# Routers of a two-block model: transposes by column half, the rank table on GpSimd, a gather part ahead of its chunks

## The chip, the cores and the metric

One core of one Trainium2 chip runs the whole program. The metric is the device time of one execution in microseconds, the median of several runs. The program computes a batch of one sequence of 256 tokens with 1024 channels, in float32.

## What is computed

A diffusion-like first block of two layers with experts, and a second block behind it. What matters here is the expert layer, which stands in both layers of the first block:

```python
h = h + m[:, :, 5] * ec_moe(modulate(rms_norm(h, norm2_g[i]), m[:, :, 3], m[:, :, 4]), *moe)
# rms_norm(x, g) = x * rsqrt(mean(x * x) + EPS) * g
# modulate(xn, shift, scale) = xn * (1 + scale) + shift
```

`ec_moe` is expert choice: a softmax over 16 experts gives each token's affinities, each expert takes the 32 tokens that like it most (of 256), runs its gate, up and down matrices (1024 x 1024 each, silu on the gate) over them, and adds the result, weighted by the affinity, to the token's row. The router is the part that ends in the choice: norm, router product, softmax, the 32 largest per expert, and the rank of each chosen token. The rest (attention and convolution in layer 0, a short convolution in layer 1, then forgetting attention, gated linear attention, cross attention and an MLP) is not touched.

## The kernel before

**The stream.** All large weights pass through `ring`, 8 slots of 2 MB in SBUF, in the order of the list `STREAM`. SyncE issues one DMA per chunk (L496 for experts, L471 for the rest) as soon as the chunk 8 places ahead has been used (`chunks_used`). The experts are 192 of its chunks: per layer four groups of four experts, per group 8 chunks of gate, 8 of up, 8 of down. In layer 0 the groups run as four loops of one, with parts of the cross attention's keys and values between them; in layer 1 they are one loop of four.

**The router** (`route(l)`, once on each of TensorE, VectorE and ScalarE) starts when the mixer's output has been added to `h`: `add_gated` (L1243, L1246) adds four quarters, column half 0 of row tiles 0 and 1, then column half 1 of both, and counts `h_ready`. TensorE transposes h (`transposes`, L1895): row tile 0 whole when three quarters are there, then row tile 1 whole after the fourth. `norm_T` counts the column pairs of which both row tiles are there. ScalarE squares both row tiles for the norm (`squares`, L580) and then evicts column pairs 1 and 3 to `xT` with the scale (`transposed`, L593); VectorE writes row tile 0 normed to `rows` (`normed_tile`, L1437), evicts pairs 0 and 2 (L1171), and writes row tile 1 normed. GpSimd turns the sums of squares into inverse roots (`rms`, L1032, L1033). When all of `xT` is there (`normed_columns`), TensorE forms the router products (L2149), four of the 8 column slices at a time in the four row groups of the array; VectorE copies the parts (L1446), TensorE adds them (L2154), VectorE applies the inverse root and the bias (L1449) and takes the maximum (L1452), ScalarE the exponential (L735), VectorE the normalization (L1454, L1455). After another transpose VectorE finds the 32 largest in four rounds (L1462, L1463), and ranks them (L1466, L1467). The rank goes back through TensorE (L2164), and VectorE writes the one-hot lists (`lists`, L1476), first those of group 0 (`mo_lists` 1), then the others, and then the rank table `RA` (L1489, two instructions, `mo_lists` 2), from which TensorE later broadcasts ranks and affinities (L2239), after the gate products of each group.

**A group** (`experts`): TensorE gathers the chosen rows in four parts of two column slices (`gather(b)`, L2219); VectorE evicts parts 0 and 2 (L1502), ScalarE parts 1 and 3 (L746), to `xsT`. The gate products read it: four chunks by `pair_chunk` (L2190), each released singly, two behind part 0 and two behind part 1; then four by `single_step` (L2211), released two at once. On TensorE's queue the order is: parts 0 and 1; chunks 0, 1; part 2; chunks 2, 3; part 3; chunks 4 to 7:

```python
gather(0)
for b in range(4):
    if b < 3:
        gather(b + 1)
    if b % 2:
        pe.wait_ge(sem("mo_xsT_act"), 2 * n + (b // 2 + 1))
    else:
        pe.wait_ge(sem("mo_xsT_dve"), 2 * n + (b // 2 + 1))
    if b < 2:
        for pair in range(2):
            pair_chunk(0, (0, 1), xsT, 0, b, pair)
single_step(0, (0, 1), xsT, 1)
```

**GpSimd's queue** around it: norm steps, loading the gate row, in layer 0 the memory rows (`mem_rows`) and then the memory norm; in layer 1 a wait for the rank table and then the DMA of `final_g` (L1080) into the place of a table that is done with.

## Time and profile before

| | |
|---|---|
| median of 3 runs | 1688.28 us (1686.38 to 1688.96) |
| span of the profiled execution | 1688.5 us |
| TensorE busy | 1483.4 us, 88% |
| TensorE weight load busy | 831.6 us, 49% |
| VectorE / ScalarE / GpSimd busy | 480.6 / 350.1 / 112.1 us |
| DMA | 562.89 MB, mean 333 GB/s over the span |
| mean granted TensorE clock | 0.961 of full speed |

Three runs and the profiled one agree within 0.2%. The page cuts the span into 40 slices of 42.2 us. The DMA's busy share is 9 tenths in nearly all slices of the first 1280 us; it dips in slice 5 (router 0 lies at 219 to 234 us) and in slices 18 and 19 (mixer and router of layer 1, the router at 825 to 841 us), and falls for good at some 1240 us, where the second block begins. TensorE's busy share is 9 nearly throughout, but it includes matmuls that run at half clock and those whose ends are modelled, so it does not say by itself that TensorE is the bound.

### The profile page before, as it was taken

What the parts mean: (1) busy time and instruction counts of PE and PEld (TensorE: products, weight loads), DVE (VectorE), ACT (ScalarE), POOL (GpSimd) and SP (SyncE); (2) the same over time, 40 slices, a digit from 0 to 9 for tenths busy, and PEclk for the clock granted to TensorE, in tenths of its full rate; (3) what the DMA queues carried; (4) which work ended last, traced back from release to release, by engine and by line L of the source; (5) the groups of instructions that cost most, each with busy time, mean ns of one, the idle gap of its engine ahead of it and who ended that gap; (6) DMA issues with size and microseconds to landing.
All of it is one profiled execution on the core that took longest, in us unless ns stands there. A gap on an engine that the chain in (4) does not pass through costs nothing. (4 is left out here: it accounts for less than half of the span.)

```text
span 1688.5 us, 18007 instructions
## 1 busy us (share of the span) xinstructions
PE 1483.4 (88%) x7708; PEld 831.6 (49%) x7708; DVE 480.6 (28%) x732; ACT 350.1 (21%) x523; POOL 112.1 (7%) x109
## 2 busy tenths in 40 slices
PE   4999979789888899789798888978878999999999
PEld 2755642232242243289532322323324867788997
DVE  1487540110100000056600100001003765336453
ACT  1122410000000000043210000000003645544442
POOL 0000000000000000010000000000002044330000
PEclk8999979989989999999899999999999999999999
DMA  9979959999999999995489999999999743334520
GB/s 373 375 316 418 396 199 429 416 402 429 416 428 428 413 409 429 415 392 202 168 364 423 427 429 423 428 428 421 429 427 364 271 168 135 121 128 174 198 100 26
DMA packets 93288, 562.89 MB, mean 333 GB/s; under 512 B 8048, under 2 KB 9448, under 8 KB 53670
## 3 DMA queue, kind: packets, MB, share of 16 engines
q1 hardware_dynamic: 89504, 551.77, 80.5%
q0 software_dynamic: 2384, 9.42, 1.6%
q8 instruction: 51, 0.84, 0.2%
q10 hardware_dynamic: 1334, 0.75, 0.2%
q14 instruction: 15, 0.12, 0.0%
HBM read 558.74 MB, written 3.17 MB: 333 GB/s over the span
## 5 line engine op out<-in xcount | busy, mean ns | idle before, releaser
L2211 PE MATMUL ps<-ring,scratch 128*32 128x512 f32 x2048 | 439.0, 609 | 63.0 <-DMA ring<-in_moe_w_up 29.6
L2211 PEld LDWEIGHTS ps<-ring,scratch 128*32 128x32 f32 x2048 | 130.7, 112 | 358.2 <-issue 351.1
L2190 PE MATMUL ps<-ring,scratch 128*32 128x512 f32 x1024 | 206.5, 607 | 28.2 <-DMA ring<-in_moe_w_down 28.2
L1930 PE MATMUL ps<-ring_parts,scratch_parts 128*128 128x512 f32 x656 | 187.0, 402 | 4.9 <-DVE xT_parts L1192 1.4
L1930 PE MATMUL ps<-scratch_parts,ring_parts 128*128 128x256 f32 x704 | 146.5, 281 | 0.0
L1930 PEld LDWEIGHTS ps<-ring_parts,scratch_parts 128*128 128x128 f32 x656 | 122.2, 189 | 33.4 <-DVE xT_parts L1192 1.6
L2190 PEld LDWEIGHTS ps<-ring,scratch 128*32 128x32 f32 x1024 | 50.6, 111 | 159.8 <-issue 109.9
L610 ACT ACTIVATE ring_parts<-ring 128x2048 fp32r<-128x2048 f32 x56 | 106.3, 1917 | 93.1 <-PE ps L1930 86.7
L461 DVE TENSOR_TENSOR ring_parts<-ring,ring_parts 128x2048 fp32r<-128x2048 f32 x46 | 105.7, 2298 | 54.9 <-ACT ring_parts L610 53.7
L1930 PEld LDWEIGHTS ps<-scratch_parts,ring_parts 128*128 128x128 f32 x704 | 116.4, 189 | 0.3
L1523 DVE TENSOR_TENSOR scratch<-ps,gate_bc 128x512 f32<-128x512 f32 x16 | 11.1, 692 | 256.8 <-PE ps L2190 256.8
L1930 PE MATMUL ps<-xT_parts,ring_parts 128*128 128x256 f32 x288 | 82.2, 286 | 1.3 <-DVE xT_parts L1183 1.3
L2219 PE MATMUL ps<-scratch,rows 128*128 128x128 f32 (+1 forms) x256 | 66.6, 421 | 14.1 <-DVE scratch L1552 5.7
L2219 PEld LDWEIGHTS ps<-scratch,rows 128*128 128x128 f32 x256 | 61.5, 327 | 32.1 <-issue 31.0
L1512 DVE TENSOR_TENSOR scratch<-scratch,ps 128x1024 f32<-128x1024 f32 x8 | 9.8, 1221 | 236.7 <-PE ps L2211 236.7
L1915 PE MATMUL ps<-ring,xT 128*128 128x512 f32 x160 | 72.9, 616 | 2.5 <-DVE xT L1171 2.5
L746 ACT ACTIVATE scratch<-ps,mod_cols,scale_cols 128x128 f32<-128x128 f32 x32 | 12.9, 453 | 276.9 <-PE ps L2219 276.9
L1930 PE MATMUL ps<-ring_parts,xT_parts 128*128 128x512 f32 x160 | 62.9, 393 | 0.0
L1508 DVE SCALAR_TENSOR_TENSOR scratch<-ps,cst,scratch 128x256 f32<-128x256 f32 x8 | 3.9, 483 | 186.9 <-ACT scratch L750 186.9
L1875 PE MATMUL ps<-ring,silu_c 128*32 128x512 f32 x384 | 50.0, 656 | 7.8 <-issue 6.9
L758 ACT ACTIVATE scratch<-ps 128x512 f32<-128x512 f32 x8 | 4.8, 597 | 246.7 <-PE ps L2245 246.7
L1930 PEld LDWEIGHTS ps<-xT_parts,ring_parts 128*128 128x128 f32 x288 | 54.2, 188 | 1.8 <-issue 1.5
(394 smaller groups left out, 1574.0 us busy)
## 6 DMA issues: line engine op xcount, KB each, us to landing
ring<-in_moe_w_gate SPq DMA_DIRECT2D x64, 2048.0 KB, 26.2
ring<-in_moe_w_up SPq DMA_DIRECT2D x64, 2048.0 KB, 15.6
ring<-in_moe_w_down SPq DMA_DIRECT2D x64, 2048.0 KB, 27.1
ring<-in_ada_w SPq DMA_DIRECT2D x24, 2048.0 KB, 14.0
ring<-in_mlp_w SPq DMA_DIRECT2D x16, 2048.0 KB, 8.5
ring<-in_sc_w_in SPq DMA_DIRECT2D x6, 2048.0 KB, 21.2
ring<-in_w_in SPq DMA_DIRECT2D x6, 2048.0 KB, 20.0
ring<-in_xattn_wkv SPq DMA_DIRECT2D x4, 2048.0 KB, 27.4
```

Source lines behind the costliest of these rows:

```text
L461: ops.tensor_tensor(lo, w, hi.bitcast(F32), ALU.subtract).then_inc(sem("w_split"), 1)
L610: nc.scalar.activation(hi, w, ACT.Copy).then_inc(sem("w_high"), 1)
L746: last = nc.scalar.activation(xsT[:, k, :], ps[:, GATHER[b], P * (k % 2):P * (k % 2 + 1)], ACT.Identity, scale=scale[:, k:k + 1], bias=shi ...
L758: nc.scalar.activation(flat(hT[:, 4:8, :]), pb(7), ACT.Copy).then_inc(sem("mo_hT_act"), 1)
L1512: nc.vector.tensor_tensor(hid, hid, ps[:, 2:4, :].rearrange("p b f -> p (b f)"), ALU.mult)\
L1523: nc.vector.tensor_tensor(ym[:, 512 * j:512 * j + 512], pb(4 + j), gate_bc[:, 512 * j:512 * j + 512], ALU.mult).then_inc(sem("mo_ym"), 1)
L1875: last = mm(ps[32 * j:32 * j + 32, bank, :], lhs, rhs, start=(c == k == 0), stop=(c == 3 and k == 1))
L1915: last = mm(ps[:, banks[t], col:col + width], lhs[:, k, P * t:P * (t + 1)], slot8(i)[:, k, 0:width], start=(k == 0), stop=(k == KD - 1))
L1930: last = mm(out, lhs[x], rhs[y], start=start and n == 0, stop=stop and n == 2)
L2190: last = mm(ps[32 * j:32 * j + 32, banks[half], :], src[:, k, CAP * j:CAP * (j + 1)], w[:, e, col:col + 512], start=(k == 0), stop=(k == K ...
L2211: last = mm(ps[32 * j:32 * j + 32, banks[half], :], src[:, k, CAP * j:CAP * (j + 1)], w[e][:, 0, col:col + 512], start=(k == 0), stop=(k = ...
L2219: last = mm(ps[:, GATHER[b], P * (k % 2):P * (k % 2 + 1)], run_slice(rows[:, t, :], k), onehot[:, t, bass.ds(g * P, P)], start=(t == 0), s ...
```

## The change

Four edits. (1) In both routers TensorE transposes by column half: half 0 of both row tiles when `h_ready` has counted two quarters, then half 1; router products of half 0 start when its evictions are done (a new semaphore `router_xT` counts them), those of half 1 wait for the others. (2) ScalarE squares row tile 1 after its evictions, VectorE evicts first, writes row tile 0 normed after that, and row tile 1 normed behind the maximum; the biased logits now wait for the inverse root of row tile 1. (3) The rank table is written by GpSimd (`rank_rows`), behind the first lists; the wait of the broadcast counts it as the third of `mo_lists`. (4) In every group the order on TensorE's queue becomes: part 0; chunks 0, 1; parts 1 and 2; chunks 2, 3; part 3; chunks 4 to 7.

```diff
@@ -571,14 +574,18 @@
+            def row_squares(name, src, junk, t, ready, count):
+
+                u = NORMS.index(name)
+                if ready:
+                    act.wait_ge(sem(ready), count)
+                nc.scalar.activation(junk, src[:, t, :], ACT.Square,
+                                     accum_out=ss[:, u, t:t + 1]).then_inc(sem("norm_ss"), 1)
+
             def squares(name, src, junk, ready=None, first=0, step=1):
...
-                u = NORMS.index(name)
                 for t in range(NT):
-                    if ready:
-                        act.wait_ge(sem(ready), first + step * t)
-                    nc.scalar.activation(junk[:, t, :], src[:, t, :], ACT.Square,
-                                         accum_out=ss[:, u, t:t + 1]).then_inc(sem("norm_ss"), 1)
+                    row_squares(name, src, junk[:, t, :], t, ready, first + step * t)
@@ -594,7 +601,7 @@
                                                         bias=shift[:, k:k + 1])
-                    last.then_inc(sem("xT_ready"), 1)
+                    last.then_inc(sem("router_xT" if name in ("moe0", "moe1") and b < 2 else "xT_ready"), 1)
@@ -728,8 +735,9 @@
                 name = f"moe{l}"
-                squares(name, h, route_junk[l], "h_ready", 4 * l + 3)
+                row_squares(name, h, route_junk[l][0], 0, "h_ready", 4 * l + 3)
                 transposed(name, xT)
+                row_squares(name, h, route_junk[l][1], 1, "h_ready", 4 * l + 4)
                 act.wait_ge(sem("mo_max"), l + 1)
@@ -1023,6 +1031,16 @@
+            def rank_rows(l):
+
+                grp = cst[0:E, C_GRP:C_GRP + GROUPS].unsqueeze(2).broadcast_to([E, GROUPS, N])
+                pool.wait_ge(sem("mo_operand"), 3 * l + 3)
+                pool.wait_ge(sem("mo_lists"), 3 * l + 1)
+                for v, src in ((0, rank), (1, affT)):
+                    last = nc.gpsimd.tensor_tensor(RA[0:E, :, v, :], src[0:E, :].unsqueeze(1).broadcast_to([E, GROUPS, N]),
+                                                   grp, ALU.mult)
+                last.then_inc(sem("mo_lists"), 1)
+
             def rms(name):
@@ -1049,6 +1067,7 @@
             pool.dma_start(mem_rows, a["mem_2"][0].rearrange("(t p) d -> p t d", p=P)).then_inc(sem("mem_in"), 16)
+            rank_rows(0)
             rms("mem")
@@ -1076,7 +1095,7 @@
             load_gate(1, 1)
-            pool.wait_ge(sem("mo_lists"), 3)
+            rank_rows(1)
             pool.dma_start(final_bc, a["final_g"].partition_broadcast(P)).then_inc(sem("final_in"), 16)
@@ -1172,7 +1191,7 @@
                                                            ALU.mult, ALU.add)
-                    last.then_inc(sem("xT_ready"), 1)
+                    last.then_inc(sem("router_xT" if name in ("moe0", "moe1") and b < 2 else "xT_ready"), 1)
@@ -1438,18 +1457,19 @@
                 dve.wait_ge(sem("h_ready"), 4 * (l + 1))
+                transposed(name, xT)
                 normed_tile(0)
-                transposed(name, xT)
-                normed_tile(1)
...
                 dve.wait_ge(sem("mo_logits"), 2 * l + 2)
+                dve.wait_ge(sem("norm_rstd"), 2 * u + 2)
                 for t in range(NT):
...
                 nc.vector.tensor_reduce(sm[:, 130:132], aff, AX.X, ALU.max, negate=True).then_inc(sem("mo_max"), 1)
+                normed_tile(1)
                 dve.wait_ge(sem("mo_exp"), 2 * l + 2)
@@ -1482,13 +1502,8 @@
                 for t in range(NT):
-                    lists(t, EG, E)
-
-                grp = cst[0:E, C_GRP:C_GRP + GROUPS].unsqueeze(2).broadcast_to([E, GROUPS, N])
-                for v, src in ((0, rank), (1, affT)):
-                    ins = nc.vector.tensor_tensor(RA[0:E, :, v, :], src[0:E, :].unsqueeze(1).broadcast_to([E, GROUPS, N]),
-                                                  grp, ALU.mult)
-                ins.then_inc(sem("mo_lists"), 1)
+                    last = lists(t, EG, E)
+                last.then_inc(sem("mo_lists"), 1)
@@ -1883,19 +1898,23 @@
+            def row_columns(name, src, t, ks):
+
+                bank = NORM_BANKS[name]
+                for k in ks:
+                    cols = run_slice(src[:, t, :], k) if name in ("moe0", "moe1") else src[:, t, P * k:P * (k + 1)]
+                    last = nc.tensor.transpose(ps[:, bank[k // 2], 256 * (k % 2) + P * t:256 * (k % 2) + P * (t + 1)],
+                                               cols, ident)
+                    if t == NT - 1 and k % 2:
+                        last.then_inc(sem("norm_T"), 1)
+
             def transposes(name, src, ready="norm_rows", first=None, step=1):
...
-                v, bank = TRANSPOSED.index(name), NORM_BANKS[name]
                 first = 2 * NORMED.index(name) + 1 if first is None else first
...
                         pe.wait_ge(sem(ready), first + step * t)
-                    for k in range(KD):
-                        cols = run_slice(src[:, t, :], k) if name in ("moe0", "moe1") else src[:, t, P * k:P * (k + 1)]
-                        last = nc.tensor.transpose(ps[:, bank[k // 2], 256 * (k % 2) + P * t:256 * (k % 2) + P * (t + 1)],
-                                                   cols, ident)
-                        if t == NT - 1 and k % 2:
-                            last.then_inc(sem("norm_T"), 1)
+                    row_columns(name, src, t, range(KD))
@@ -2142,10 +2161,15 @@
                 name = f"moe{l}"
-                transposes(name, h, "h_ready", 4 * l + 3)
-                normed_columns(name)
+                for half in range(2):
+                    for t in range(NT):
+                        pe.wait_ge(sem("h_ready"), 4 * l + (3 + t if half else 2))
+                        row_columns(name, h, t, range(4 * half, 4 * half + 4))
+                pe.wait_ge(sem("router_xT"), 2 * l + 2)
                 for k in range(KD):
                     j = k % 4
+                    if k == 4:
+                        normed_columns(name)
                     last = mm(ps[32 * j:32 * j + 32, 0, 0:N], lf[:, E * (k + 7 * l):E * (k + 7 * l) + 32], xT[:, k, :],
@@ -2166,7 +2190,7 @@
                 pe.wait_ge(sem("norm_rows"), 2 * NORMED.index(name) + 2)
-                pe.wait_ge(sem("mo_lists"), 2 * l + 1)
+                pe.wait_ge(sem("mo_lists"), 3 * l + 1)
@@ -2224,7 +2248,9 @@
                     for b in range(4):
-                        if b < 3:
+                        if b == 1:
+                            gather(1)
+                        if 1 <= b < 3:
                             gather(b + 1)
@@ -2235,7 +2261,7 @@
-                    pe.wait_ge(sem("mo_lists"), 2 * l + 2)
+                    pe.wait_ge(sem("mo_lists"), 3 * l + 3)
                     mm(pb(4), cst[0:E, C_E4:C_E4 + P], RA[0:E].rearrange("e g v n -> e (g v n)")[:, bass.ds(g * 2 * N, 2 * N)],
```

Left out above: `route_junk` becomes pairs of single-row buffers, and the counts of `xT_ready` are tabled in `COLUMNS_READY`, since two of four evictions of each router now count elsewhere.

## Rows read from the trace of the kernel before

**Rows 1.** Stretches by time: busy us of each engine, clock, DMA share, GB/s.
```profile
860.00:1000.00 140.00, 123.30 (x565) 41.23 (x564) 8.48 (x14) 9.68 (x14) 0.00 (x0) 0.95 1.01 426
...
231.00:243.00 12.00, 9.18 (x44) 5.45 (x46) 6.13 (x13) 0.81 (x2) 0.00 (x0) 0.60 0.04 17
```

**Rows 2.** SyncE's issues in group 0 of layer 0: start, us, line, what.
```profile
243.01 0.33 SPq L496 DMA_DIRECT2D ring<-in_moe_w_up  x1
...
262.19 0.81 SPq L496 DMA_DIRECT2D ring<-in_moe_w_up  x2
```

**Rows 3.** Single issues to landing: 243.0; fifth at 262.2, 388.6, 868.0, 511.6.
```profile
ring<-in_moe_w_up SPq DMA_DIRECT2D x1, 2048.0 KB, 7.8
...
ring<-in_moe_w_up SPq DMA_DIRECT2D x1, 2048.0 KB, 8.8
...
ring<-in_moe_w_up SPq DMA_DIRECT2D x1, 2048.0 KB, 9.0
...
ring<-in_moe_w_up SPq DMA_DIRECT2D x1, 2048.0 KB, 9.7
...
ring<-in_moe_w_up SPq DMA_DIRECT2D x1, 2048.0 KB, 12.0
```

**Rows 4.** Instructions in time order: start, us, what, count, idle before; router 0, router 1.
```profile
219.20 1.06 ACT L580 ACTIVATE rows<-h 128x1024 f32<-128x1024 f32 x1 [1.60 <-DVE h L1246]
219.20 0.75 DVE L1437 TENSOR_SCALAR rows<-h,rstd 128x1024 f32<-128x1024 f32 x1
...
219.22 1.23 PE L1895 MATMUL ps<-cst,h 128*128 128x128 f32 x8 [0.56 <-DVE h L1246]
219.87 1.66 DVE L1171 TENSOR_SCALAR xT<-ps,scale_cols 128x256 f32<-128x256 f32 x4
...
220.26 1.55 ACT L593 ACTIVATE xT<-ps,scale_cols 128x256 f32<-128x256 f32 x4
...
221.86 1.07 PE L2149 MATMUL ps<-xT,router_w 128*32 128x256 f32 x16 [1.41 <-ACT xT L593]
...
224.55 0.38 DVE L1449 SCALAR_TENSOR_TENSOR scratch<-ps,rstd,small 128x16 f32<-128x16 f32 x2 [1.13 <-PE ps L2154]
...
827.83 1.94 PE L2149 MATMUL ps<-xT,router_w 128*32 128x256 f32 x16 [1.41 <-ACT xT L593]
```

**Rows 5.** The same view: GpSimd's last norm step, VectorE behind the exponential, router 0.
```profile
220.71 0.54 POOL L1033 TENSOR_TENSOR rstd<-ms,mhalf 128x1 f32<-128x1 f32 x1
...
225.91 0.17 DVE L1454 RECIPROCAL small<-small 128x2 f32<-128x2 f32 x1 [0.76 <-ACT scratch L735]
```

**Rows 6.** The same view: gather and first chunk in router 0, group 1, router 1.
```profile
234.21 4.07 PE L2219 MATMUL ps<-scratch,rows 128*128 128x128 f32 x16 [1.05 <-DVE scratch L1476]
234.82 2.34 DVE L1489 TENSOR_TENSOR scratch<-scratch,cst 16x1024 f32<-16x1024 f32 x2
237.09 0.71 DVE L1502 TENSOR_SCALAR scratch<-ps,scale_cols,mod_cols 128x128 f32<-128x128 f32 x2
238.21 6.51 PE L2190 MATMUL ps<-ring,scratch 128*32 128x512 f32 x32
...
362.89 0.73 DVE L1502 TENSOR_SCALAR scratch<-ps,scale_cols,mod_cols 128x128 f32<-128x128 f32 x2 [2.37 <-PE ps L2219]
...
841.28 4.00 PE L2219 MATMUL ps<-scratch,rows 128*128 x16 [1.29 <-DVE scratch L1476]
```

**Rows 7.** Stretches at half granted clock (the third number from the end).
```profile
223.40:240.60 17.20, 8.41 (x30) 5.67 (x32) 10.81 (x31) 2.78 (x7) 0.60 (x1) 0.50 0.42 124
...
827.60:844.60 17.00, 7.28 (x38) 5.23 (x39) 11.73 (x32) 3.44 (x7) 1.20 (x2) 0.50 0.35 133
```

**Rows 8.** GpSimd's groups and single instructions, and the broadcast on TensorE.
```profile
L1107 POOL TENSOR_TENSOR scratch<-scratch,gate_bc 128x1024 f32<-128x1024 f32 x1 | 3.6, 3590 | 5.8 <-ACT scratch L897 5.8
...
841.10 0.53 POOL L1080 DMA_DIRECT2D scratch<-in_final_g  x1 [12.83 <-DVE scratch L1476]
...
267.28 1.12 PE L2239 MATMUL ps<-scratch,cst 16*128 16x512 f32 x2
```

More of the change, by code:

```diff
@@ L398, in build @@
         cw1 = gcol[:, 6:6 + SCK, :].rearrange("p j c -> p c j")
+        COLUMNS_READY = {}
+        for name in TRANSPOSED:
+            COLUMNS_READY[name] = sum(2 if n in ("moe0", "moe1") else 4 for n in TRANSPOSED[:len(COLUMNS_READY) + 1])
         PARAMS = 7
```

6 lines of the change are left out of this document (3 added, 3 removed).

## The prediction

> **What bounds the kernel now.** I read the DMA share by stretch first, then the loading queue, then the two routers instruction by instruction. The change touches the two routers and the start of each expert group, so the question is what a microsecond there is worth. Through layer 1's experts the 16 DMA engines are never free: share 1.01 and 426 GB/s over 140 us [rows 1], while TensorE has idle time. A 2048 KB chunk then takes 4.9 us (2.10 MB by 426 GB/s), and TensorE waits for chunks. The stream stands still in one kind of place: a router uses no expert chunk, so once the eight ring slots are full nothing can be loaded. Before 243.0 us the share is 0.04 for 12 us [rows 1]. It starts again when the first gate chunk of group 0 has been used: the queue issues at 243.01 [rows 2]. So a router's length counts only through the moments at which it lets the queue go on, and whatever the stream wins there it keeps, because after it the stream is the bound until late in layer 1.
>
> The first release is not the only such moment. After 243.01 four chunks are released one by one, and the fifth and sixth together at 262.19 [rows 2], because `single_step` counts two at once. Four chunks are 4 x 4.9 = 19.6 us of transfer, and the fifth release comes 19.2 us after the first: the stream is just kept fed. A chunk issued to an empty queue lands 7.8 us later [rows 3]. There are four places where the ring restarts close to empty: router 0, layer 0's groups 1 and 3, router 1. The fifth chunk lands 8.8, 9.0 and 9.7 us after its issue in the first, second and fourth [rows 3], and 8.9 in group 3, which repeats group 1. So in these places the fifth release could come only 1.0, 1.2, 1.1 and 1.9 us later before it delays the stream. I call this the slack; the argument hangs on it.
>
> **The change part by part.** *Router chain, layer 0.* Now ScalarE squares the second row tile (1.06 us) before its two evictions, and VectorE writes a normed tile (0.75) before its own; the evictions end at 221.8 and router products start at 221.86 [rows 4]. In the new order the first column half is transposed and ScalarE evicts its part while the last addition to h is still running; after 219.2 there are left four transposes (half of the 1.23 us), VectorE's four evictions (1.66, started at 219.2 in place of 219.87) and ScalarE's last two (half of 1.55, from 219.9). Evictions end at 220.9, 0.95 earlier, and the first half of the products is done by then, so 0.5 of their 1.07 us goes too. The copy of the partial logits, which now follows the products' end at 222.93, waits for their new end (221.5) and for the normed tile, moved behind the evictions (220.9 + 0.75 = 221.7). Gain 1.3 us. The moved squares start at 220.8 and need their 1.06 us, the read of the sum (0.2) and GpSimd's two steps (until 221.25 after a start at 219.20, 2.05 us in all): the inverse root is there at 222.9. It is first needed by the biased logits at 224.55 - 1.3 = 223.2: hidden by 0.3 us, and each further delay of the squares would cost in full. The second normed tile (0.75) moves into the wait for the exponentials, which is 0.76 long [rows 5]: nothing, at most 0.1. The exp table load follows the squares at 222.1 for 1.28 us and ends before the maximum (223.8): nothing.
>
> *Router chain, layer 1.* The same, but here products run 1.94 us instead of 1.07 [rows 4], since the granted clock falls to half at 827.6 [rows 7]. Starting 0.95 earlier, they end about there and take the short time: 0.95 + 1.94 - 0.55 = 2.3, less 0.1 for the normed tile, 2.2 us. If the clock falls earlier instead it is 1.3 to 1.4.
>
> *Rank table to GpSimd.* It takes two instructions, 2.34 us, off VectorE, directly ahead of the eviction of gather part 0 (237.09) [rows 6]. Now that delay is covered by gather part 1; with the new gather order it would not be, so this part is needed for the next. On GpSimd no row shows this shape; the nearest with a broadcast input is 3.6 us for 128x1024 [rows 8], so 5 to 7.2 us for both, from 234 to about 241. TensorE needs it at 267.3 [rows 8]: free, with 25 us of room. Behind it on GpSimd's queue wait, in layer 0, only the memory norms of group 1. In layer 1 the DMA of final_g moves from 841.1 [rows 8] to about 845, close to the stream's restart: 0.5 MB, 0 to 1.2 us if they meet; I take 0.
>
> *Gather order, every group.* Now: part 0, part 1 (4.0 us together), then the first chunk at 238.21 [rows 6]. New: part 0 (2.05), then nothing to do for TensorE until VectorE has evicted it, 0.73 us as in group 1, where VectorE is free and starts at once [rows 6], then the chunk: 3.0 us after the gather's start instead of 4.0. The first chunk starts 1.0 earlier. Part 1 follows after two chunks, so the third chunk comes 1.1 later and everything behind it 0.85 later (the exposed eviction). The work until the fifth release is the same plus this gap: **the fifth release loses 0.85 us against the gather's start**, where there is 1.0 to 1.9 of slack.
>
> *The clock.* In both routers the gather begins at half clock, and full clock comes back at 240.6, 6.4 us after its start at 234.21 [rows 6, 7], and at 844.6, 3.3 us after 841.28. A gather part takes 2.0 to 2.1 us at either level, but chunks take twice the time at half: now they run cold for 240.6 - 238.2 = 2.4 and 0 us, a loss of 1.2 and 0. In the new order chunks start a microsecond earlier into the cold (0.5 more), and the gap of 0.85 us lies in the midst of the burst that brings the clock back. If the return counts from the work behind the gap (3.3 to 6.4 us after the first chunk) the loss is 1.7 to 3.2, on average 1.9 more than now. Nothing in this trace shows such a gap; the bounds are 0.5 and 3 us, and I take 1.5, between them, for each of the four places. In the other groups the fifth chunk waits in a full queue, 12.0 us from issue to landing in layer 0's group 2 [rows 3] and longer in layer 1's, where the ring is full: 4 us or more of room (12.0 - 7.8), and what TensorE loses there costs nothing.
>
> **The sum.** Change at the fifth release = 0.85 + 1.5 = 2.35 us later against the gather's start; less slack, less what the router chain saved. Router 0: 2.35 - 1.0 - 1.3 = 0.05. Group 1: 2.35 - 1.2 = +1.15. Group 3: 2.35 - 1.1 = +1.25. Router 1: 2.35 - 1.9 - 2.2 = -1.75. Total +0.7 us. The profiled execution's span is 1688.5 us and the median of the runs 1688.28, so no correction is due: 1688.3 + 0.7 = 1689.0. A change that shortens both routers is worth nothing, because the stream is let go by the fifth release and not by the first.
>
> A rule of the Trainium skill, TensorE: Matmul & The Clock Gate (Part 1: The HAM clock gate), speaks against the change: the throttle is the default and only sustained activity releases it, so a hole in the burst is paid at half clock. It also says that the number of cold matmuls differs between runs of one kernel and that the ramp is under 1% of a typical kernel; by it rival B holds, with a scatter that I can't place. DMA: Bandwidth & Descriptors (Anatomy of one DMA) gives a fixed cost of about 2.0 us plus bytes by 436 GB/s, 6.8 us for a lone chunk, for another issuing path; by that the slack would be 1 us larger in each place and the time, as an estimate, 1686. The row shows 7.8 (the same in router 1 and group 3) and decides.
>
> **The rivals.** *A, the router's gain comes through whole.* If the clock comes back at the same moment as now, the fifth release is 1.35 later against the gather (2.15 in router 1, which now has no cold chunk): router 0 -1.0, groups 1 and 3 +0.15 each, router 1 -1.8: 1685.8. If besides the first release governs everywhere (four chunks are enough lead), routers give 1.8 and 1.9 and groups 1 and 3, where the first release finds the queue all but empty too, 0.5 to 0.8 each (1.0 less half of what chunks run longer cold): 5 us, 1683.3. For it: the share is 1.00 between 243 and 262 and there is slack. Against: the slack is smaller than gap and cold chunks together.
>
> *B, the gap holds the clock down (slower).* Full clock then comes 6.4 us after the first chunk: extra 3, at the fifth release 3.85 later: router 0 +1.55, group 1 +2.65, group 3 +2.75, router 1 -0.25: +6.7, 1695.0; with half of the places so, 1691.9. It decides against the change when full clock returns more than some 8.5 us after the gather's start. For it: half clock lasts through 17 us of scattered work in both routers [rows 7]. Against: one gap of 0.85 us is short.
>
> *C, the change does not do what it says:* TensorE may reach the first half late, since its queue still holds the mixer's last products, or the squares reach the biased logits late. Each takes up to 0.5 us of the router gain: 1689.5 to 1690. It stays in the forecast's range.
>
> **How the numbers follow.** Forecast with C 0.70: 1689.0, own range 1686.5 to 1691.5. A 0.15 (its whole form 0.08). B 0.15. The range that leaves out 2 in 10 reaches from A's milder form to B's with half of the places: 1685.2 to 1692.3. A measurement of this kernel can tell some 0.2% (3.4 us) from no change: faster by more needs A's whole form or a router gain beyond my count, 0.12; slower by more needs B, 0.14; within it 0.74.
>
> **What would show it.** Right: router products in two bursts, the partial-logits copy earlier against the last addition to h by 1.3 us in layer 0 and 2.2 in layer 1; an idle time of TensorE of about 0.8 us between gather part 0 and the first chunk; the first `in_moe_w_up` issue 1 to 2 us earlier against the last addition to h, the fifth later against the first by 2.1 to 3.5 us; the landings of the fifth chunk 7.8 to 8 us after its issue. Wrong: a fifth chunk landing 9 us or more after its issue (then the first release governs, A), full clock unchanged against the gather's start (A) or later than 8.5 us (B), a wait of the rank products on GpSimd, or DMA share under 1.00 between restarts.

## The result, and the profile after

The changed kernel is slower by about a quarter of a per cent.

| | before | after |
|---|---|---|
| median of 16 runs each | 1687.76 us (1683.25 to 1689.81) | 1691.72 us (1688.53 to 1693.67) |
| ratio | | 1.0028 (95% interval 1.0020 to 1.0036) |
| span of the profiled execution | 1688.5 us | 1690.1 us |
| last addition to h to gather, router 0 / router 1 | 15.04 / 16.14 us | 13.38 / 13.41 us |
| GpSimd busy | 112.1 us | 120.0 us |
| mean granted TensorE clock | 0.961 | 0.964 |

The forecast was +0.7 us (1689.0). The medians differ by 4.0 us, the ratio is worth 4.7 us. The two profiled spans differ by 1.7 us only, but the profiled execution of after happened to be 1.6 us ahead when router 0 began (last addition to h ending at 217.59 instead of 219.17), so I compare stretches and not positions.

The page of after: its busy times, and the groups of the first gate chunks and of the gather.

```profile
PE 1487.6 (88%) x7708; PEld 829.6 (49%) x7708; DVE 479.7 (28%) x728; ACT 350.5 (21%) x523; POOL 120.0 (7%) x113
...
L2214 PE MATMUL ps<-ring,scratch 128*32 128x512 f32 x1024 | 215.4, 628 | 37.2 <-DMA ring<-in_moe_w_down 30.2
...
L2243 PE MATMUL ps<-scratch,rows 128*128 128x128 f32 (+1 forms) x256 | 66.5, 413 | 14.1 <-DVE scratch L1567 5.7
```

The products of `pair_chunk`, the first behind each gather, take 628 ns each on average; in the kernel before they took 607 (206.5 us in all). More of them run at half clock: 64 of the 1024 take over 1 us, where 20 did before.

Router 0 and the gather behind it, after, in order of time (start, us, engine, line, what, count, idle before). These rows answer [rows 4 to 6].

```profile
216.90 0.69 DVE L1265 TENSOR_TENSOR h<-h,xT 128x512 f32<-128x512 f32 x1
217.19 0.84 ACT L600 ACTIVATE xT<-ps,scale_cols 128x256 f32<-128x256 f32 x2 [1.17 <-PE ps L1906]
217.63 1.66 DVE L1190 TENSOR_SCALAR xT<-ps,scale_cols 128x256 f32<-128x256 f32 x4
...
218.56 1.42 PE L2173 MATMUL ps<-xT,router_w 128*32 128x256 f32 x16 [0.17 <-DVE xT L1190]
...
219.16 1.06 ACT L582 ACTIVATE rows<-h 128x1024 f32<-128x1024 f32 x1
...
220.05 0.42 DVE L1464 COPY scratch<-ps 128x256 f32<-128x256 f32 x1
...
220.53 0.62 PE L2178 MATMUL ps<-small,scratch 128*128 128x16 f32 x4 [0.55 <-DVE scratch L1464]
220.67 0.54 POOL L1051 TENSOR_TENSOR rstd<-ms,mhalf 128x1 f32<-128x1 f32 x1
...
221.32 0.38 DVE L1468 SCALAR_TENSOR_TENSOR scratch<-ps,rstd,small 128x16 f32<-128x16 f32 x2 [0.84 <-POOL rstd L1051]
...
230.25 3.13 DVE L1496 TENSOR_TENSOR scratch<-cst,scratch 128x128 f32<-128x128 f32 x4
230.89 4.24 POOL L1040 TENSOR_TENSOR scratch<-scratch,cst 16x1024 f32<-16x1024 f32 x2 [7.46 <-DVE scratch L1496]
...
230.98 2.20 PE L2243 MATMUL ps<-scratch,rows 128*128 128x128 f32 x8 [1.05 <-DVE scratch L1496]
233.30 0.72 DVE L1517 TENSOR_SCALAR scratch<-ps,scale_cols,mod_cols 128x128 f32<-128x128 f32 x2
...
234.07 7.80 PE L2214 MATMUL ps<-ring,scratch 128*32 128x512 f32 x32 [0.89 <-DVE scratch L1517]
```

What to see: ScalarE begins to evict xT while the last addition to h runs; the copy of the partial logits starts 2.46 us after that addition's end (220.05 - 217.59). Before it was 3.83 after. The two rows of before behind that number, and behind the sum of the parts below:

```profile
223.00 0.42 DVE L1446 COPY scratch<-ps 128x256 f32<-128x256 f32 x1 [0.81 <-PE ps L2149]
...
223.48 1.04 PE L2154 MATMUL ps<-small,scratch 128*128 128x16 f32 x4 [0.55 <-DVE scratch L1446]
```

In the kernel after, TensorE idles 0.89 us between gather part 0 and the first chunk, which starts 3.09 us after the gather. The first two chunks take 7.80 us against 6.51 in [rows 6].

The same two marks in router 1.

```profile
825.99 0.69 DVE L1265 TENSOR_TENSOR h<-h,xT 128x512 f32<-128x512 f32 x1
...
829.14 0.42 DVE L1464 COPY scratch<-ps 128x256 f32<-128x256 f32 x1
...
840.10 2.23 PE L2243 MATMUL ps<-scratch,rows 128*128 x8 [1.28 <-DVE scratch L1496]
```

Again 2.46 us, here against 4.70 before (the copy then started at 829.84, the last addition to h ended at 825.14). From the last addition to h to the gather this pair of executions gives 1.66 and 2.73 us, 4.4 in all. How much router 1 gives depends on the execution of before that it is held against, because the clock does not fall at the same moment in each: in dose1 (below), whose router 1 is the old one, the router products still ran at full clock,

```profile
827.57 1.07 PE L2149 MATMUL ps<-xT,router_w 128*32 128x256 f32 x16 [1.41 <-ACT xT L593]
```

against 1.94 us in [rows 4]. The five kernels with the old routers (before, gather_and_rank, dose1, dose2, dose4) took 14.41 to 15.04 us over router 0 and 14.65 to 16.14 over router 1, means 14.90 and 15.48; the nine with the new ones took 13.37 to 13.43 and 13.41 to 13.62. On average the routers thus gave 1.5 and 2.0 us, 3.5 in all. The loss is in what follows.

Stretches of 6 us around the issue of the fifth chunk (2 us ahead of it to 4 us behind it) in after: router 0, group 1, group 3, router 1. Columns as in [rows 1]; the last two are the DMA share and GB/s.

```profile
259.21:265.21 6.00, 6.00 (x38) 1.83 (x36) 0.00 (x0) 0.00 (x0) 0.00 (x0) 1.00 0.86 325
386.44:392.44 6.00, 6.00 (x38) 1.83 (x36) 0.00 (x0) 0.00 (x0) 0.00 (x0) 1.00 0.90 330
648.08:654.08 6.00, 6.00 (x38) 1.82 (x36) 0.00 (x0) 0.00 (x0) 0.00 (x0) 1.00 0.91 347
867.61:873.61 6.00, 6.00 (x38) 1.83 (x36) 0.00 (x0) 0.00 (x0) 0.00 (x0) 1.00 0.82 319
```

And the same stretch of group 1 in the kernel before:

```profile
386.56:392.56 6.00, 6.00 (x38) 1.82 (x36) 0.00 (x0) 0.00 (x0) 0.00 (x0) 1.00 1.01 431
```

The stream moved 426 GB/s when full [rows 1]. At 325 GB/s, 6 us lack 6 x (1 - 325/426) = 1.42 us of stream; the four rows of after lack 1.42, 1.35, 1.11 and 1.51, mean 1.35. The four stretches of before (426, 431, 431, 421 GB/s) lack nothing, mean 0.0. I call this **the hole**. TensorE is at work in it (6.00 of 6.00 us busy), so TensorE's busy time does not show it. It costs time later, because the stream is the bound.

The issues of after around it, in group 1: the fourth and the fifth chunk, and the landing times after issue.

```profile
378.38 0.33 SPq L499 DMA_DIRECT2D ring<-in_moe_w_up  x1
...
388.44 0.33 SPq L499 DMA_DIRECT2D ring<-in_moe_w_up  x1
...
ring<-in_moe_w_up SPq DMA_DIRECT2D x1, 2048.0 KB, 12.8
...
ring<-in_moe_w_up SPq DMA_DIRECT2D x1, 2048.0 KB, 10.1
```

The fourth chunk lands at 391.2, the fifth at 398.5, 7.3 us later where a full stream takes 4.9. The stretch that lies mostly ahead of the fourth landing, and the one behind it:

```profile
388.50:391.50 3.00, 3.00 (x16) 0.82 (x14) 0.00 (x0) 0.00 (x0) 0.00 (x0) 1.00 0.74 224
391.50:396.00 4.50, 4.50 (x20) 1.13 (x18) 0.48 (x1) 1.30 (x2) 0.00 (x0) 1.00 1.01 415
```

The stream is at half its rate while the fourth chunk is still landing, and full again behind it. The first issue of this group is at 367.39, the fifth 21.05 us behind it; before it was 19.18 behind in all four places.

The third issue comes later as well, 9.2 us behind the first instead of 7.4. Two chunks are 9.8 us of transfer, so by the same reckoning it is still in time, and the 6 us around it lack nothing (426, 429, 421 and 421 GB/s in the four places). Group 1:

```profile
374.63:380.63 6.00, 5.78 (x34) 2.87 (x30) 0.00 (x0) 0.19 (x1) 0.00 (x0) 1.00 1.03 429
```

### The profile page after: what moved, and what is told of

Read it like the earlier page. It is cut to its first block and busy times, and to the rows that moved or that the text cites. A ratio compares the mean times of both kernels' runs of the same rounds, so it can differ in the third digit from the quotient of the medians.

```text
span 1690.1 us, 18009 instructions
## 1 busy us (share of the span) xinstructions
PE 1487.6 (88%) x7708; PEld 829.6 (49%) x7708; DVE 479.7 (28%) x728; ACT 350.5 (21%) x523; POOL 120.0 (7%) x113
## 5 line engine op out<-in xcount | busy, mean ns | idle before, releaser
L2235 PE MATMUL ps<-ring,scratch 128*32 128x512 f32 x2048 | 438.4, 609 | 54.6 <-DMA ring<-in_moe_w_up 24.9
L2214 PE MATMUL ps<-ring,scratch 128*32 128x512 f32 x1024 | 215.4, 628 | 37.2 <-DMA ring<-in_moe_w_down 30.2
L766 ACT ACTIVATE scratch<-ps 128x512 f32<-128x512 f32 x8 | 4.8, 597 | 243.0 <-PE ps L2271 243.0
```

The source lines that it names most:

```text
L766: nc.scalar.activation(flat(hT[:, 4:8, :]), pb(7), ACT.Copy).then_inc(sem("mo_hT_act"), 1)
L2214: last = mm(ps[32 * j:32 * j + 32, banks[half], :], src[:, k, CAP * j:CAP * (j + 1)], w[:, e, col:col + 512], start=(k == 0), stop=(k == K ...
L2235: last = mm(ps[32 * j:32 * j + 32, banks[half], :], src[:, k, CAP * j:CAP * (j + 1)], w[e][:, 0, col:col + 512], start=(k == 0), stop=(k = ...
```

## The experiments

Each ratio is to the kernel before, run beside it. Three marks are read in each of the four places (router 0, groups 1 and 3 of layer 0, router 1) and given as means: the first issue after the gather's start (before 8.39 us), the fifth issue after the first (before 19.18), and the fifth landing after the gather's start (before 36.68; after 38.93). The hole is read as above. The table in the next section has them all. All expectations but the last were written before the hole was understood; "lead" in them is the time from the fifth chunk's issue to the fourth's landing.

**The gather order undone.** After, with edit 4 alone taken back:

```diff
-                        if b == 1:
-                            gather(1)
-                        if 1 <= b < 3:
+                        if b < 3:
                             gather(b + 1)
```

> The changed kernel with the old order of gather parts; router edits and the rank table on GpSimd stay. Theory 1 (the gather order costs, because it moves the fifth release of a group 1.85 us and more against the first, and the stream runs dry in the four places where the ring restarts close to empty): the router chain's 1.6 us (layer 0) and 2.7 us (layer 1), read from the changed kernel's trace, come through whole: 4.3 us faster than before, ratio 0.9974; fifth release 19.2 us behind the first as before. Rival 2 (the router edits or GpSimd's interference cost the time): no faster than before, ratio 1.000 or more.

Measured 0.9977 (0.9967 to 0.9987): 3.9 us faster than before, 8.6 faster than after. The first three edits are a gain and the fourth turns it into a loss. It also speaks against the prediction's sentence that a shorter router is worth nothing: 4.3 us of router (3.5 against the mean of the old routers) became 3.9 us of time.

**Edits 3 and 4 without the others.** Before, with the rank table on GpSimd and the new gather order.

> The kernel before with the new gather order and the rank table on GpSimd, no router edits. Theory 1: all of the loss and none of the gain: 4.0 + 4.3 = 8 us slower than before, ratio 1.005. My prediction's slack (1.0, 1.2, 1.1, 1.9 us, with 2.35 later at the fifth release) would give +4.2 us, 1.0025. Rival 2: within 0.1% of before.

Measured 1.0039 (1.0027 to 1.0052), +6.6 us. Fifth issue 21.04 after the first, fifth landing at 39.10, holes of 1.2 us. The slack model's 1.0025 lies just below the interval.

**The new order in layer 1 only.** After, with `if l == 1` around the new order.

> The changed kernel with the new gather order in layer 1 alone; layer 0 has the old one. Theory 1: of the four places only router 1's is left, where the fifth chunk lands some 2.5 us later against the gather's start; layer 1's other groups have a full ring and pay nothing: 2 to 3 us slower than the changed kernel with the old order everywhere (0.9977), so 0.9990 to 0.9995. If the loss came from every group (TensorE's own time): four of eight groups, half of 7.5 us, 0.9999. If it came from layer 0 alone: 0.9977.

Measured 0.9994 (0.9984 to 1.0003). Group 3 of layer 0 (old order) and router 1 (new order):

```profile
638.32:644.32 6.00, 6.00 (x38) 1.83 (x36) 0.00 (x0) 0.00 (x0) 0.00 (x0) 1.00 1.00 423
...
858.00:864.00 6.00, 6.00 (x38) 1.83 (x36) 0.00 (x0) 0.00 (x0) 0.00 (x0) 1.00 0.91 347
```

One place of four has the new order close to an empty ring, and it alone has the hole (347 GB/s, 1.11 us). The other three groups of layer 1 have the new order too, with a full ring, and their chunks land 4.9 us apart, with 423 to 429 GB/s around the fifth issue: there the order costs nothing, as predicted.

**The routers alone.** After, with the old order and the rank table back on VectorE.

> The changed kernel with the old gather order and the rank table back on VectorE: the router edits alone. Theory 1: the rank table is worth nothing where gather part 1 covers it, on either engine: the same as with the table on GpSimd, 0.9974 to 0.9980. Rival: GpSimd's table doubles the time of the other lists on VectorE (1.0 to 2.7 us in the changed kernel's trace) and that costs in the old order too: this one faster by 1 us or more, under 0.997.

Measured 0.9977 (0.9966 to 0.9987), the same as with the table on GpSimd. With the old gather order it is worth nothing where the table is built; with the new order no run has it on VectorE. It changes how long the lists take, though; VectorE in this kernel:

```profile
228.37 1.43 DVE L1485 TENSOR_TENSOR scratch<-cst,scratch 128x128 f32<-128x128 f32 x4
```

The same four instructions took 3.13 us in after, beside GpSimd's table. All of the difference is in the fourth, which starts 0.24 us behind GpSimd's first product:

```profile
231.13 2.25 DVE L1496 TENSOR_TENSOR scratch<-cst,scratch 128x384 f32<-128x384 f32 x1
```

In router_only it takes 0.55 us. GpSimd's two products take 2.07 us (beside this list) and 2.19 (the second runs on for 1.7 us after the list's end), so VectorE is what is slowed. The gather waits for the first list only; in after the fourth ends at 233.38, where the eviction of gather part 0 begins, so a longer one would have delayed the first chunk.

**More work between the first and the fifth release.** Before, with half of gather part 3 multiplied once more next to part 3 (dose 1), or all of it (dose 2, `(0, 1)` for `(0,)`); the values written are those that stand there.

```diff
                     for b in range(4):
+                        if b == 2:
+                            gather(3, (0,), False)
                         if b < 3:
                             gather(b + 1)
```

> The kernel before; half of gather part 3 (one column slice) is multiplied twice in every group: the fifth release comes 1.05 us later against the first. Slack as I predicted it (1.0, 1.2, 1.1, 1.9): it swallows the delay, 0 to 0.1 us slower, ratio 1.000. No slack (the fifth chunk must be issued 3.9 us or more before the fourth lands, and before it just was): landings of the fifth chunk 1 us later in the four places, 4 us slower, ratio 1.0025.

> The kernel before; gather part 3 of every group is multiplied twice (the same products into the same place), so that the fifth release comes 2.1 us later against the first, and nothing before it moves. Slack as I predicted it (1.0, 1.2, 1.1, 1.9): +1.1 +0.9 +1.0 +0.2 = 3.2 us slower, ratio 1.0019. Theory 1 in its sharper form (no slack; a chunk issued while the previous one is in its last 3 us leaves a hole of up to 2.5 us, as in the changed kernel's trace at 388 and 870 us): 2.1 to 2.5 us in each of four places, 8.4 to 10 us slower, ratio 1.005 to 1.006.

Measured 1.0016 (1.0004 to 1.0028) and 1.0043 (1.0031 to 1.0055). Both lie above the slack model (1.000 and 1.0019), though this edit makes no gap, leaves the routers alone and does not move the third issue (7.37 us behind the first, as before). So the slack was wrong, whatever the gap does to the clock. Group 1 of dose 1 and of dose 2:

```profile
385.16:391.16 6.00, 6.00 (x38) 1.83 (x36) 0.00 (x0) 0.00 (x0) 0.00 (x0) 1.00 0.98 377
```
```profile
386.40:392.40 6.00, 6.00 (x38) 1.83 (x36) 0.00 (x0) 0.00 (x0) 0.00 (x0) 1.00 0.95 358
```

**The wait that holds the fifth release, moved.** The fifth and sixth chunks are multiplied with all four column slices of parts 2 and 3; only the last two need part 3's eviction. In the kernel with the gather order undone, the wait goes there:

```diff
                                 for kk in range(RUN):
+                                    if c0 == 0 and pair == half == 0 and kk == 2:
+                                        pe.wait_ge(sem("mo_xsT_act"), 2 * n + 2)
...
-                        if b % 2:
-                            pe.wait_ge(sem("mo_xsT_act"), 2 * n + (b // 2 + 1))
-                        else:
+                        if b == 1:
+                            pe.wait_ge(sem("mo_xsT_act"), 2 * n + 1)
+                        elif b % 2 == 0:
```

> The changed kernel with the old gather order, and TensorE waits for the eviction of gather part 3 only before the third column slice of chunks 4 and 5, the first that reads it. The fifth release comes 0.8 us earlier against the first (18.3 instead of 19.2). Theory 1 with a threshold near 3.9 us of lead: the fifth chunk follows the fourth without a hole in both, so little: 0 to 1 us faster than 0.9977, ratio 0.9971 to 0.9977. If the fifth release sets the stream's restart one to one: 0.85 us in each of four places, 3.4 us faster, 0.9957.

Measured 0.9973 (0.9961 to 0.9985), not to be told from 0.9977 without it. The fifth issue comes 18.18 behind the first instead of 19.19; where that was early enough already, the microsecond buys nothing. The same edit on after:

> The changed kernel, with TensorE waiting for the eviction of gather part 3 only before the third column slice of chunks 4 and 5. The fifth release comes 0.9 to 1.0 us earlier against the first (20.0 instead of 21.0), its lead over the fourth landing grows from 2.7 to 3.6 us. No slack below 3.6 to 3.9 us of lead: the holes shrink by 1 us and more in four places, 4 to 6 us faster than the changed kernel, 0.9990 to 1.0004. With my prediction's model of a landing (7.8 us after the issue, whatever the lead): 4 x 0.9 = 3.6 us faster, 1.0007.

Measured 0.9996 (0.9983 to 1.0008), 5.4 us faster than after. The fifth issue is 20.01 behind the first, the holes are 0.26 us. Here the same microsecond is worth its length in all four places (4.1 us); that it is worth more is within the scatter, as the two intervals leave some 3 to 8 us. Group 1 of this kernel, to be read beside group 1 of after:

```profile
383.84:389.84 6.00, 6.00 (x38) 1.74 (x36) 0.00 (x0) 0.00 (x0) 0.00 (x0) 1.00 1.01 407
```

**The gap filled.** After, with half of gather part 1 in the gap between part 0 and the first chunk, and the other half at its new place:

```diff
                     gather(0)
+                    gather(1, (0,))
                     for b in range(4):
                         if b == 1:
-                            gather(1)
+                            gather(1, (1,))
```

> The changed kernel, but half of gather part 1 (one of its two column slices) is multiplied in the time in which TensorE waits for the eviction of part 0. The gap of 0.9 us goes, the fifth release comes 0.9 to 1.1 us earlier than in the changed kernel, the first at most 0.2 later. Theory 1: holes of the stream shrink, 3 to 4 us faster than the changed kernel: 0.9999 to 1.0007 against before. Prediction's rival A (first release governs): as the changed kernel, 1.003. If the hole in the burst is what holds the clock down: full clock within 6.4 us of the gather's start, and the time near 0.999.

Measured 0.9982 (0.9972 to 0.9991), better than either theory had it. The half part is moved out from between first and fifth release (20.12) and it also brings the clock back earlier. To part the two, the same half is multiplied in the gap for nothing and again at its place:

> The changed kernel with useless work in TensorE's gap: half of gather part 1 is multiplied there and then again in its usual place, so the work up to the fifth release is not shortened, the gap alone is filled. If the gap costs only its own length: fifth release against the gather's start as in the changed kernel (29.3 to 30.4 us, mean 29.9) or 0.1 later, ratio 1.003. If the gap also keeps the clock down (theory 1 and my rival B): full clock 1 to 2.5 us earlier against the gather's start, the fifth release 0.5 to 1.0 us earlier (29.0), ratio 1.0005 to 1.002.

Measured 1.0016 (1.0002 to 1.003), 2.0 us faster than after (1.0028) by the point estimates, though the intervals overlap. (The profiled execution of this kernel, 1697.0 us, was the slowest of its twelve, whose median is 1690.2.) Where the clock comes back is clear, however. Two stretches each of router 0, after and then this kernel (the third number from the end is the granted clock):

```profile
231.00:239.00 8.00, 7.11 (x24) 3.02 (x28) 3.02 (x4) 0.00 (x0) 4.13 (x2) 0.50 0.00 0
239.10:241.80 2.70, 2.70 (x21) 0.58 (x13) 0.00 (x0) 0.00 (x0) 0.00 (x0) 1.00 0.53 97
```
```profile
232.60:237.00 4.40, 4.40 (x16) 3.16 (x18) 2.99 (x4) 0.00 (x0) 4.09 (x2) 0.50 0.00 0
237.20:241.00 3.80, 3.80 (x28) 1.15 (x26) 0.00 (x0) 0.00 (x0) 0.00 (x0) 1.00 0.09 17
```

After: the gather starts at 230.98 and full clock is there 8.1 us later; with the gap filled it starts at 232.55 and full clock comes 4.5 us later. The means over the four places are 7.3, 7.2 and 7.6 us in the three kernels with the gap, 5.5 to 5.6 in the three with the gap filled, and 4.6 to 6.2 in those of the old order. A gap of 0.9 us holds the clock down for some 1.8 us more on average; single places overlap (6.2 to 8.9 us with the gap, 4.5 to 6.4 with it filled).

The dummy kernel's router 0 had its fifth issue 22.75 us behind the first, not 21.05. The granted clock says why: between first and fifth issue, behind the last gather part, it fell to half once more, for 3.4 us, in which TensorE does 1.7 us less work (21.05 + 1.70 = 22.75).

```profile
254.20:257.50 3.30, 3.30 (x10) 0.97 (x8) 0.00 (x0) 0.00 (x0) 0.00 (x0) 0.50 0.96 407
```

In after the same moments ran at full clock, with the same instructions behind the first issue; why it fell here is open. It serves as a larger dose in that place: 213 GB/s over the 6 us, a hole of 3.0 us.

**Both mends.** After, with the gap filled and the wait moved.

> Both mends together, the version that should beat the others: half of part 1 in the gap, and the late wait for part 3. Fifth release 19.1 to 19.2 us behind the first as in the kernel before, the first 0.5 to 1.0 us earlier against the gather's start than with the old order. Theory 1: lead of the fifth chunk 4 us, no hole there, third chunk's lead 4.9: 1 to 3 us faster than the old order (0.9977), ratio 0.996 to 0.9975. If the first release is worth nothing: 0.9977, as late_wait.

Measured 0.9965 (0.9953 to 0.9978), 1681.0 us: faster than both kernels. No gap, and no hole:

```profile
232.75 3.14 PE L2245 MATMUL ps<-scratch,rows 128*128 128x128 f32 x12 [1.05 <-DVE scratch L1496]
235.07 0.72 DVE L1517 TENSOR_SCALAR scratch<-ps,scale_cols,mod_cols 128x128 f32<-128x128 f32 x2
...
235.84 6.11 PE L2214 MATMUL ps<-ring,scratch 128*32 128x512 f32 x32
```
```profile
382.83:388.83 6.00, 6.00 (x38) 1.74 (x36) 0.00 (x0) 0.00 (x0) 0.00 (x0) 1.00 1.00 426
```

Its interval overlaps those of 0.9973 and 0.9977, so it is not shown that the new order adds anything over the old once both mends are in.

**A test of the new reading.** By then the holes stood against the fifth issue after the first as follows: none at 18.2 and 19.2 us, 0.26 at 20.0, 0.7 at 20.1, 0.9 to 1.5 at 21.0 (means by kernel 1.2 to 1.35). Four chunks are 4 x 4.9 = 19.6 us of transfer. A last kernel takes part 3 twice more:

> The kernel before, with part 3 of the gather multiplied three times over (the two extra passes write what stands there anyway), ahead of chunks 2 and 3's place in every group: the fifth release moves from 19.2 us behind the first to 19.2 + 4 x 0.93 = 22.9 us (21.05 with one extra pass). It tests a reading that the runs so far suggest: what counts is not how long the fifth chunk takes from issue to landing, but whether four chunks (4 x 4.9 = 19.6 us of transfer) last until the fifth comes; beyond 19.6 each microsecond is a microsecond in which the DMA engines have nothing, one for one, in each of the four places where the ring restarts close to empty. That theory expects a shortfall of the stream of 22.9 - 19.6 = 3.3 us in each place, read as 4 x (1 - GB/s / 427) over some 5 us around the fifth issue, and 4 x 3.3 = 13 us in all: ratio 1.0075 to 1.0085. The slack theory of the prediction (1.0, 1.2, 1.1 and 1.9 us free) expects 4 x 3.7 - 5.2 = 9.6 us: 1.0057. A theory by which the hole has a fixed size (landings 2.4 us late once the lead is short, as with one extra pass) expects no more than one extra pass costs: 1.0043 to 1.005.

Measured 1.0082 (1.0063 to 1.0101), as the new reading expected. Slack (1.0057) and a hole of fixed size (up to 1.005) lie outside. Group 1:

```profile
392.39:398.39 6.00, 6.00 (x38) 1.82 (x36) 0.00 (x0) 0.00 (x0) 0.00 (x0) 1.00 0.58 183
```

The fifth issue is 22.92 behind the first here, the holes are 3.7, 3.4, 2.9 and 3.4, mean 3.35 us. In router 0 it is 24.61: there too the clock was at half for 3.4 us on the way (0.50 over 256.20 to 259.50). For so late an issue the 6 us are too short a stretch; 16 us around it (8 on each side) moved 293 GB/s, that is they lack 16 x (1 - 293/426) = 5.0 us, which is 24.61 - 19.6.

```profile
256.73:272.73 16.00, 16.00 (x76) 4.68 (x74) 0.48 (x1) 1.73 (x3) 0.00 (x0) 0.91 0.73 293
```

## Why the prediction was wrong

**The step that failed is the slack, the term of -5.2 us in the sum.** The prediction had both halves of the right argument in its first part: four chunks are 19.6 us of transfer, the fifth release comes 19.2 after the first, "the stream is just kept fed". That leaves 0.4 us. It then took another measure: a chunk issued to an empty queue lands 7.8 us after issue [rows 3], the fifth lands 8.8 to 9.7 after, so 1.0 to 1.9 us are free. A landing is the end of the chunk's last piece, and the stream runs dry before that: in group 1 of after the stream moves 224 GB/s from 388.5 us on, while the fourth chunk lands at 391.2. The time from issue to first data stands ahead of the first chunk as well as the fifth, so by this reading it drops out of the difference. What counts is the fifth issue after the first, less 19.6:

| kernel | fifth issue after first | that less 19.6, mean | hole, mean | first issue after gather | change of 4 x (first issue + hole) | change of the routers | sum | measured |
|---|---|---|---|---|---|---|---|---|
| late_wait | 18.18 | none | 0.00 | 8.07 | -1.3 | -4.3 | -5.6 | -4.6 |
| gap_filled_late | 19.11 | none | 0.00 | 7.99 | -1.6 | -4.3 | -5.9 | -5.9 |
| old_gather | 19.18 | none | 0.04 | 8.21 | -0.6 | -4.3 | -4.9 | -3.9 |
| router_only | 19.19 | none | 0.08 | 8.05 | -1.0 | -4.3 | -5.3 | -3.9 |
| layer1_order | 19.19, once 21.05 | 1.45 once | 0.32 | 8.16 | +0.4 | -4.4 | -4.0 | -1.0 |
| changed_late | 20.01 | 0.4 | 0.26 | 8.96 | +3.3 | -4.4 | -1.1 | -0.7 |
| gap_filled | 20.12 | 0.5 | 0.68 | 7.93 | +0.9 | -4.1 | -3.2 | -3.0 |
| dose1 | 20.12 | 0.5 | 0.73 | 8.77 | +4.4 | -1.5 | +2.9 | +2.7 |
| after | 21.04 | 1.4 | 1.35 | 8.83 | +7.2 | -4.4 | +2.8 | +4.7 |
| gather_and_rank | 21.04 | 1.4 | 1.18 | 8.75 | +6.2 | -0.7 | +5.5 | +6.6 |
| dose2 | 21.05 | 1.45 | 1.32 | 8.21 | +4.6 | -0.3 | +4.3 | +7.3 |
| gap_dummy | 21.05, once 22.75 | 1.9 | 1.55 | 8.01 | +4.7 | -4.3 | +0.4 | +2.7 |
| dose4 | 22.92, once 24.61 | 3.7 | 3.35 | 8.10 | +12.2 | -1.5 | +10.7 | +13.8 |

All in us and means over the four places; the changes are against the kernel before (first issue 8.39, no hole, routers 31.18 together), and measured is (ratio - 1) x 1687. For after: 4 x (8.83 - 8.39 + 1.35) = 7.2, and 7.2 - 4.4 = 2.8. The signs agree in all thirteen rows and the sums miss by up to 3.1 us (1.4 on average), mostly too low where there are holes. A sum from the landings of the fifth chunk instead (9.0 - 4.4 = 4.6 for after) is no better over all rows: 1.5 us on average, up to 4.6 in dose4. Why the last landing moves by up to 1 us a place more than the hole is open. Three things limit such sums. Each is read from one profiled execution, while the measured column is a median of runs that scatter by 2 to 12 us. The router column is held against one execution of before, whose router 1 was the longest of five. And an earlier first issue can be worth its length only where the stream had stopped: in group 1 of late_wait, old_gather, router_only, layer1_order and dose2 it had not (390 to 431 GB/s in the 3.6 us behind the first issue, 244 before). So the table shows which way and about how much; the size of a microsecond in it is not shown to better than some 3 us in all.

Put back into the prediction: (2.35 - 0.4) x 4 - 3.5 = +4.3 us, against 4.0 to 4.7 measured. One term was wrong and the rest held:

- *Router 0 and 1.* Copy of the partial logits earlier by 1.37 (predicted 1.3) and 2.24 (2.2). Another 0.3 and 0.5 came unforeseen: the sum of the parts (L2178) now takes 0.62 us, against 1.04 before, since the clock has not yet fallen. Total 4.4 for 3.5 in this pair of executions; against the mean of the five old routers it is 3.5, and that the moment at which the clock falls moves from execution to execution was not in the prediction.
- *Squares hidden.* Barely: the biased logits are put down to GpSimd's inverse root in both routers, with 0.84 and 0.85 us of idle time. But most of that is the parts' sum, which ends at 221.15; the root ends at 221.21, so it costs 0.1.
- *Gap.* 0.89 us, first chunk 3.09 after the gather (predicted 0.85 and 3.0).
- *Clock.* The cold chunks cost more than before: the first issue moved by +0.44 against the gather on average, though its chunk starts 0.91 earlier, which makes 1.35 us a place (predicted 1.5). Kernels that are alike up to this issue differ by as much (8.05 to 8.77 us in the seven with the old gather order, 8.75 to 8.96 in the three with the gap in every group); their means, 8.26 and 8.85, give 1.5. It showed in the sentence "fifth later against the first by 2.1 to 3.5", which was wrong: the cold stretch lies ahead of the first issue, and between first and fifth only gather part 1 has come in, 1.86 us. The sum at the fifth release is nonetheless right: 2.29 us later on average, for 2.35.
- *Full ring.* Right: layer 0's group 2 and layer 1's groups 1 to 3 lost nothing (423 to 429 GB/s around the fifth issue in after).
- *Rank table.* Two instructions of 2.1 us, 4.2 in all (bounds 5 to 7.2, too high), and nobody waits. `final_g` is issued at 843.96, ahead of the restart at 848.56: no collision.
- *Fifth landing.* "9 us or more after its issue" was meant as a sign of rival A. It came in two of the four places (10.1 and 9.7; the others 8.8 and 7.7), and did not mean A: the chunks were issued as the stream ran dry. Before had 8.8 to 9.7 with no hole at all [rows 3], so the number could not tell the two apart.

**Rival A** falls. The first issue came earlier against the last addition to h, by 1.25 us in layer 0 and 1.86 in layer 1; this was worth its length in old_gather, where the fifth issue follows in time, and was eaten by the hole in after. Neither release governs alone: the first sets when the stream begins, the fifth whether it goes on. (Its 2.15 us for router 1 does not follow from its rows, full clock 3.3 us and the first chunk 3.0 us after the gather; nothing here rests on it.) **Rival B** named the right sign and, with half of its places, nearly the right time (1691.9), but by the wrong road: full clock came 8.1, 6.2, 8.5 and 6.5 us after the gather, never past its 8.5. What the longer cold stretch costs is 1.35 us a place, and was in the forecast's sum. The Trainium skill, TensorE: Matmul & The Clock Gate (Part 1: The HAM clock gate), says that the throttled state is the default and that activity releases it; the prediction concluded from it that a hole in the burst is paid at half clock, and the filled gap agrees: full clock 8.1 us after the gather with the hole against 4.5 without, in router 0. **Rival C** falls, the routers do what they say.

The Trainium skill, DMA: Bandwidth & Descriptors (Anatomy of one DMA), gives about 2.0 us plus bytes by 436 GB/s, for another issuing path; the 6.8 us that this makes for a lone chunk, an estimate, would have made the slack larger still and the time 1685 by the prediction's own sum (it says 1686). The runs went the other way, and a lone chunk took 7.7 us in router 0 of after.

## What to carry to other kernels

When a ring restarts close to empty, compare the time between its first release and each later one with the transfer time of what was released in between, and spend none of the rest: landing times hide that the stream runs dry before the last piece lands. Work put between two releases costs about one for one beyond that point (0.7 us of stream at 0.5 over, 1.35 at 1.4, 5.0 at 5.0), in every such place, even while TensorE shows no idle time; the view to read is the DMA share and GB/s of the few microseconds around the late issue. A short idle time in the burst that brings the clock back is best filled with work that is due soon anyway.

## What the runs showed of the hardware

- The stream's hole opens about when the late chunk is issued, not at the last landing of the chunk before: 224 GB/s over 388.5 to 391.5 with the fourth landing at 391.2 and the fifth issue at 388.44. How work is spread over the 16 engines in it is open.
- A 2048 KB chunk issued into a stream that runs dry took 7.7 to 10.1 us in after, one to an empty queue 7.7 to 7.9 (routers 0 and 1 of before and after).
- 0.9 us of idle time on TensorE, behind the first part of the gather, moved the return of full clock by some 1.8 us on average (7.2 to 7.6 us after the gather in the three kernels with it, 5.5 to 5.6 in the three with it filled), by 3.5 in router 0.
- The moment at which the granted clock falls in unchanged code is not fixed: router 1's products took 1.07 us in dose1 and dose4, 1.94, 1.89 and 1.68 in before, gather_and_rank and dose2; and in router 0 of gap_dummy and dose4 it was at half for 3.4 us behind the last gather part, where the other kernels kept full clock, which moved the fifth issue by 1.7 us.
- GpSimd's 16x1024 product took 2.1 us against 1.17 on VectorE (half of 2.34, [rows 6]). Of VectorE's four lists the one of 128x384 that ran beside it took 2.25 us against 0.55, and ended 0.4 us after GpSimd's first product did. The Trainium skill, GPSIMD Engine Reference (section 1, Specifications), says that the two engines share their SBUF interfaces where VectorE has two inputs, as the lists have; the runs agree for VectorE. GpSimd was not slowed to be seen: its product beside the list took 2.07 us, the next, with the list gone for most of it, 2.19.
